# A two-layer encoder trunk on one core: the first FFN input product in two halves of the features, with modulation units 1024 wide

## The reference, cut to what matters

```python
cond = silu(c)
for layer in range(2):
    mod = cond @ w_ada[layer] + b_ada[layer]        # 2048 x 12288, 100 MB a layer
    sh_m, sc_m, g_m, sh_f, sc_f, g_f = split(mod, 6)
    h = rms_norm(x, norm_mix_gain[layer]) * (1 + sc_m) + sh_m
    y = pool_mixer(h) if layer == 0 else hgrn2_mixer(h)   # hgrn: w_in 2048 x 8192, w_out 2048 x 2048
    x = x + g_m * y
    h = rms_norm(x, norm_ffn_gain[layer]) * (1 + sc_f) + sh_f
    a, b = split(h @ w_ffn_in[layer], 2)            # 2048 x 11264
    x = x + g_f * ((silu(a) * b) @ w_ffn_out[layer])      # 5632 x 2048
return rms_norm(x, final_gain)
```

## Time and profile before

| what | us |
| --- | --- |
| median of 3 runs | 2437.61 (2435.35 to 2439.57) |
| the profiled execution | 2439.01, of which the span from first to last instruction is 2437.3 |
| PE busy | 2180.4 (89%), 9905 matmul instructions |
| DVE busy | 1743.5 (72%) |
| ACT busy | 1077.3 (44%) |
| DMA | 573.63 MB, mean 235 GB/s |

### The profile page before, as it was taken

How to read it: one execution, slowest core, us unless ns; L and a number is a source line. 1 busy time by engine, 2 the same in 40 slices (tenths; PEclk the granted TensorE clock), 3 DMA queues, 4 the chain that set the end, 5 groups by cost and what they waited for, 6 DMA issues and landing times. The chain is left out here.

```text
span 2437.3 us, 33187 instructions
## 1 busy us (share of the span) xinstructions
PE 2180.4 (89%) x9905; PEld 1786.8 (73%) x9905; DVE 1743.5 (72%) x2673; ACT 1077.3 (44%) x1803; POOL 9.8 (0%) x43
## 2 busy tenths in 40 slices
PE   1284279999999999989999999898999999999997
PEld 1243268888888787877878787776888888878886
DVE  6868867777776688875969686987555555557675
ACT  2021044444444444445555545544545444444443
POOL 0000000000000000010000000000000000000000
PEclk9997579999999999999999999998999999999999
DMA  8978958888887798975656564685666666667775
GB/s 303 323 247 288 316 161 286 268 276 286 269 275 252 242 325 311 323 248 181 187 168 200 177 188 133 193 298 188 190 191 183 192 185 191 189 214 255 253 257 201
DMA packets 295002, 573.63 MB, mean 235 GB/s; under 512 B 17504, under 2 KB 17632, under 8 KB 294160
## 3 DMA queue, kind: packets, MB, share of 16 engines
q1 hardware_dynamic: 294928, 572.76, 71.9%
HBM read 570.59 MB, written 2.10 MB: 235 GB/s over the span
## 5 line engine op out<-in xcount | busy, mean ns | idle before, releaser
L1041 DVE TENSOR_TENSOR w_lo<-raw,w_hi 128x512 fp32r<-128x512 f32 x1392 | 941.9, 688 | 571.2 <-ACT w_hi L738 566.4
L738 ACT ACTIVATE w_hi<-raw 128x512 fp32r<-128x512 f32 x1392 | 850.8, 629 | 741.9 <-PE prod L484 716.1
L482 PE MATMUL prod<-w_hi,h_hi 128*128 128x512 f32 x2080 | 830.6, 399 | 25.9 <-DVE w_lo L1041 20.4
L484 PE MATMUL prod<-w_hi,h_lo 128*128 128x512 f32 x2080 | 815.2, 392 | 0.0
L483 PE MATMUL prod<-w_lo,h_hi 128*128 128x512 f32 x2080 | 814.6, 392 | 0.0
L482 PEld LDWEIGHTS prod<-w_hi,h_hi 128*128 128x128 f32 x2080 | 393.8, 189 | 123.9 <-DVE w_lo L1041 37.4
L484 PEld LDWEIGHTS prod<-w_hi,h_lo 128*128 128x128 f32 x2080 | 392.9, 189 | 84.1
L483 PEld LDWEIGHTS prod<-w_lo,h_hi 128*128 128x128 f32 x2080 | 393.7, 189 | 79.2 <-issue 1.4
L1075 DVE SCALAR_TENSOR_TENSOR acc<-ada,cond,acc 128x512 f32<-128x512 f32 x536 | 393.5, 745 | 18.3 <-DMA ada<-in_w_ada 16.9
L482 PE MATMUL prod<-w_hi,g_hi 128*128 128x512 f32 x704 | 278.7, 396 | 3.0 <-DVE w_lo L1041 3.0
L484 PE MATMUL prod<-w_hi,g_lo 128*128 128x512 f32 x704 | 274.8, 390 | 0.0
(11 more groups left out here) (124 smaller groups left out, 982.0 us busy)
## 6 DMA issues: line engine op xcount, KB each, us to landing
ada<-in_w_ada SPq DMA_DIRECT2D x384, 512.0 KB, 5.2
raw<-in_w_ffn_in SPq DMA_DIRECT2D x352, 512.0 KB, 4.4
raw<-in_w_ffn_out SPq DMA_DIRECT2D x176, 512.0 KB, 4.9
raw<-in_hgrn_w_in SPq DMA_DIRECT2D x128, 512.0 KB, 3.8
raw<-in_hgrn_w_out SPq DMA_DIRECT2D x32, 512.0 KB, 5.0
raw<-in_pool_w SPq DMA_DIRECT2D x8, 512.0 KB, 7.0
xs<-in_x SPq DMA_DIRECT2D x2, 1024.0 KB, 9.7
out<-xs SPq DMA_DIRECT2D x2, 1024.0 KB, 4.0
```

What stands on the lines that cost most here:

```text
L482: pe.matmul(o, hi(k)[:, ts], wh, start=(k == 0), stop=False)
L484: mm = pe.matmul(o, lo(k)[:, ts], wh, start=False, stop=(k == blocks - 1))
L738: act.activation(split_slot(t, deep)[0], raw[:, r, t.get("step") % 2], ACT.Copy).then_inc(hi_ready, 1)
L1041: dve.tensor_tensor(wl, raw[:, r, t.get("step") % 2], wh, ALU.subtract).then_inc(lo_ready, 1)
```

## The change

The modulation units become 1024 columns wide (24 in all, `UW`): one load is 128 rows x 4 KB, again 512 KB, one fold is 128x1024 into one buffer, and every fold after the first waits for the one before it. The order of the units changes. Eight wide units come ahead of the first FFN (list `HEAD`: shift and scale of the mixer by halves, both gate halves, then only the first half of the FFN's shift and scale). Sixteen are folded behind products at written step numbers (`BEHIND`): 8 in the first FFN, 5 and most of a sixth in HGRN, the rest of that in its output product, 2 in the second FFN.

The first FFN input product runs in two halves of the features. For the first 9 of 11 column groups (`NA`), 18 chunks of 8 steps use features 0 to 1023 and ACT copies each to SBUF (`part_gate`, `part_value`); meanwhile the other half of shift and scale is folded. Then 18 chunks of 8 steps use features 1024 to 2047, and DVE adds the parts (`add_gate`, `add_value`). The last 2 groups run in whole chunks. The work per step on PE is the same.

Weight splits are made on pairs: one ACT and one DVE instruction for 128x1024, a ring of four pairs in every stage. The pooling groups are put between folds, PE multiplies 8 of 16 blocks of the two wide gate units (32 blocks of 512). The transposes of the last hidden group move into the first chunk of the FFN output. All hardware loops are gone; every wait is on a constant.

```diff
-    PE_LOADS = [6] * (NCH - 1) + [KU - ADA]
-    AHEAD = SPL
+    PE_FOLDS = 8
+    AHEAD = 4
+    NA = 9
+    EVAC = 5
...
+    HEAD = [(0, SH_M, 0), (0, SC_M, 0), (0, SH_M, 1), (0, SC_M, 1), (0, G_M, 0), (0, G_M, 1), (0, SH_F, 0), (0, SC_F, 0)]
+
+    BEHIND = [((0, SH_F, 1), A0 + 2, A0 + 50, None), ((0, SC_F, 1), A0 + 56, A0 + 106, A0 + 116),
+              ((0, G_F, 0), A0 + 118, A0 + 172, None), ((1, SH_M, 0), A0 + 180, A0 + 234, None),
+              ((1, SH_M, 1), A0 + 242, A0 + 296, None), ((1, SC_M, 0), A0 + 304, OUT0 + 6, None),
+              ((1, SC_M, 1), OUT0 + 14, OUT0 + 68, None), ((0, G_F, 1), OUT0 + 76, OUT0 + 132, OUT0 + 144),
+              ((1, SH_F, 0), H0 + 20, H0 + 62, None), ((1, SH_F, 1), H0 + 68, H0 + 110, None),
+              ((1, SC_F, 0), H0 + 116, H0 + 158, None), ((1, SC_F, 1), H0 + 164, H0 + 204, None),
+              ((1, G_M, 0), H0 + 210, H0 + 246, None), ((1, G_M, 1), H0 + 254, W0 + 32, W0 + 43),
+              ((1, G_F, 0), OUT1 - 116, OUT1 - 60, None), ((1, G_F, 1), OUT1 + 46, OUT1 + 84, OUT1 + 110)]
...
-            def hi(deep=False):
+            def hi():
...
-                act.activation(split_slot(t, deep)[0], raw[:, r, t.get("step") % 2], ACT.Copy).then_inc(hi_ready, 1)
+                act.activation(w_hi[:, slot], raw[:, r], ACT.Copy).then_inc(hi_ready, 1)
...
+            for c2 in range(2 * NA):
+                def in_a(k):
+                    if c2 == 0:
+                        first_half(k)
+                    second_features()
+                    if c2 and k == EVAC:
+                        take(C_A + c2 - 1, part_of(C_A + c2 - 1), ACT.Copy)
+                chunk(in_a, AHEAD if c2 == 0 else 0)
...
+            def add_gate(j):
+                multiplied(dve, C_B + 2 * j)
+                if j:
+                    dve.wait_ge(small_full[1], t.get("small1"))
+                dve.tensor_tensor(tok[:, :, :], prod[0][:, :, :], part_gate[:, j], ALU.add).then_inc(prod_free[0], 1)
+
+            def add_value(j):
+                multiplied(dve, C_B + 2 * j + 1)
+                pv = part_value[:, j]
+                dve.tensor_tensor(pv, prod[1][:, :, :], pv, ALU.add).then_inc(prod_free[1], 1)
+                dve.wait_ge(silu_ready, j + 1)
+                evacuated(dve, C_B + 2 * j + 1)
+                dve.tensor_tensor(tok[:, :, :], tok[:, :, :], pv, ALU.mult).then_inc(hidden_ready, 1)
```

More of the change, by code:

```diff
@@ L52, in tick @@
         self.n[name] = self.get(name) + k
[L54 to L74, removed]
 def due(step, n, first, last):
@@ L341, in load_chunk @@
-            def load_chunk(src, at, blocks, units=(), shift=0, loaded=0):
-                for s in range(blocks):
-                    if s % 2 == 0 and s >= loaded:
[L345 to L348, removed]
+                    if u:
+                        sp.wait_ge(unit_summed, 2 * u)
+                    for r in range(2):
+                        sp.dma_start(bias[32 * r:32 * r + 1, :],
+                                     b_ada[layer:layer + 1, at + r * CH:at + (r + 1) * CH]).then_inc(bias_loaded, 16)
@@ L507, in reduce_unit @@
[L507 to L520 removed]
+                        after(s)
@@ new lines, in product, with h_product, multiply_loads @@
+                    for u, (_, last) in SPAN.items():
+                        if g == last + SUM:
+                            reduce_unit(u)
+                t.tick("chunk")
+            def h_product(after=None, before=None, first=0):
+                product(h_hi, h_lo, first, after, before)
+            def multiply_loads(u):
+                pe.wait_ge(unit_taken, u)
+                for k in range(PE_FOLDS):
+                    n = u * KD + k
+                    slot = n % ADA
+                    pe.wait_ge(ada_loaded[slot], 16 * (n // ADA + 1))
+                    for o in range(2):
+                        mm = pe.matmul(modp[:, o], cond_rows[:, k], ada[:, slot, o * CH:(o + 1) * CH], start=(k == 0), stop=False)
+                    mm.then_inc(ada_free[slot], 1)
@@ L741, in ahead, with chunk @@
             def ahead():
-                for k in range(AHEAD):
+                for _ in range(AHEAD // 2):
                     hi()
-            def chunk(n, before=None, deep=False, done=0):
-                for k in range(n):
+            def chunk(before=None, done=0):
+                for k in range(STEPS[t.get("chunk")]):
+                    for u, at in TAKE.items():
+                        if t.get("step") == at:
+                            take_unit(u)
                     if before is not None:
@@ new lines, in chunk, with take_unit @@
+                    t.tick("step")
+                t.tick("chunk")
+            def take_unit(u):
+                layer, section, half = UNITS[u]
+                act.wait_ge(unit_reduced, u + 1)
+                if is_gate(u):
+                    earlier = sum(is_gate(v) for v in range(u))
+                    if earlier:
+                        act.wait_ge(x_updated, 2 * earlier)
+                    act.activation(gate[:, :, :], modp[:, :, :], ACT.Copy).then_inc(unit_taken, 1)
+                    return
+                at = (KD if section in (SC_M, SC_F) else 0) + half * UB
+                act.activation(mod[:, 0 if section < SH_F else 1, at:at + UB], modp[:, 0, 0:UB], ACT.Copy).then_inc(unit_taken, 1)
@@ L989, in _ @@
             ahead()
[L990 removed]
+            take(C_WOUT - 1, sg[:, :, :], ACT.Silu)
             t.tick("small0", NL // 2)
@@ L1044, in ahead, with chunk @@
             def ahead():
-                for k in range(AHEAD):
+                for _ in range(AHEAD // 2):
                     lo()
-            def chunk(n, after=None, deep=False, done=0, before=None):
-                for k in range(n):
+            def chunk(after=None, done=0, before=None):
+                for k in range(STEPS[t.get("chunk")]):
                     if before is not None:
                         before(k)
-                    if k >= done:
-                        lo(deep)
+                    if k >= done and k % 2 == 0:
+                        lo()
@@ L1089, in unit @@
-            def unit():
-                for k in range(KD):
-                    fold(k)
-            def norm_prepare(gains, branch):
-                if gains is not None:
-                    dve.wait_ge(unit_taken, t.value("unit"))
-                    dve.scalar_tensor_tensor(gain[:, :], mod[:, branch, KD:2 * KD], 1.0, cols[:, gains:gains + KD],
-                                             ALU.add, ALU.mult)
-                dve.wait_ge(squared, t.value("sq"))
+                    for span in SPAN.values():
+                        for _ in due(t.get("step"), KD, *span):
+                            fold()
@@ L1190, in _, with pool_group @@
             t.tick("sq", NCH * TB)
-            unit()
-            unit()
-            with t.loop(dve, NCH - 1, PER_2UNITS):
-                unit()
-                unit()
-            def pool_group(n, w):
+            def pool_group(n, w, between):
                 src, span, lo_end = padded, 1, 1
-                step = [t.get("pool")]
                 def done(ins):
@@ new lines, in _ @@
+            normalise(3, 1)
+            for _ in range(HG):
+                lo()
+            pool_group(2, WINDOWS[2], nothing)
+            pool_group(3, WINDOWS[3], fold)
+            folds(KD - PE_FOLDS - 7)
+            pool_update(0)
+            pool_update(1)
+            for _ in range(HG):
+                lo()
+            folds(KD - PE_FOLDS)
+            folds(4)
+            pool_update(2)
+            folds(2)
+            pool_update(3)
+            folds(4)
+            norm_root()
```

1155 lines of the change are left out of this document (566 added, 589 removed).

## The result

The kernel after the change takes 2406.86 us (median of 4 runs, 2405.55 to 2407.36), against 2438.59 before in the same runs: a ratio of 0.987, 95% interval 0.9853 to 0.9887. It is faster by 1.3%. 2355 was forecast with a range of 2322 to 2402, so the time lies 5 us above the range and the gain is 32 us of 82. The profiled execution has a span of 2405.6 us.

The account below looks back on a forecast made before the run. The prediction took PE as the bound from 329.6 us on and the modulation units' four-slot load ring in the head. Stages 262 + 500 + 256 + 474 + 114 + 493 + 242 + 14 gave 2355 us, range 2322 to 2402.

Parts of the forecast that it names:

- The head: Start to first FFN product: 262 us, 68 us earlier, by folding 8 wide units, 16 of the old ones, not 20.
- The reading that the ring of four slots sets the pace: Head: load landing plus folds limit the four-slot ring to 1.58 us a load, 25.3 us a wide unit.
- The cross-check by bytes, 263 us: Head: loads of 75.4 MB at the old mean rate of 287 GB/s give 263 us.
- 3 us for stalls: First FFN input: allowance added to 497 us of PE work, giving 500.
- Sum 19.6, 86%: Second halves of first FFN input: DVE work of 19.6 us in 16 steps, 22.8 us of PE.
- the term of 12 us: HGRN: time added because DVE would be 90% busy, in a stage forecast at 474 us against 459.5 before.
- The bounds I gave were 0 and 45: HGRN's added time: 0 if PE hides 90% DVE load as it hides 79%, 45 if the ceiling is 80%.
- The row that I had: Old HGRN output product: two chunks with DVE busy 87% took 53.4 us where PE's own work is 45.3.
- The sign that I had named for being wrong: Second halves or HGRN: PE waiting on `w_lo` for over 20 us in all would show the forecast wrong.
- The rival that code loading would cost 0.7 us a block: Whole span: some 130 blocks of straight code loaded; at 0.7 us each the time is 2446 us; slower, chance 0.04.
- the restarts of the loop go: Second FFN output: with the loop unrolled its restarts vanish, 242 us against 246.5 before.
- DVE binds in HGRN and the second halves: Rival: DVE ceiling at 80 to 85% adds 20 to 45 us in HGRN, 5 to 15 in FFN; 2380 to 2415; chance 0.24.

Follow-up runs that it names:

- e9: Changed kernel with the two halves undone: all ten shift and scale units folded in the head, first FFN input in whole chunks; 2437.2 us, 0.998 of before.
- e4: Changed kernel, second halves of first FFN input reordered: ACT takes hidden blocks at steps 4 and 5, DVE makes their low parts after the gate addition; 2389.2 us.
- e5: e4 with ACT copying the turned q and f blocks in HGRN one step later, after that step's weight split; 2378.1 us, HGRN 494.1.
- e2: Changed kernel with folds of the five units inside HGRN on 64 of 1024 columns, except each unit's first; 2384.8 us, HGRN 480.9.
- e3: e2 with weight splits on single steps in place of pairs; 2368.5 us in a single run, HGRN 471.2.
- e12: Changed kernel with late hidden blocks, later q and f copies in HGRN, single-step splits, and HGRN folds on 64 columns; 2351.1 us, HGRN 464.4.
- e11: e5 with one unit moved from HGRN to the first FFN output and the other four spread wider, pair splits kept; 2365.6 us, 0.9689 of before.

## Why the prediction was wrong, by its steps

**The head (262, measured 266.9): right.** The wide fold was put at 1.28 us and is 1279 ns:

```profile
L1016 DVE SCALAR_TENSOR_TENSOR acc<-ada,cond,acc 128x1024 f32<-128x1024 f32 x292 | 373.5, 1279 | 9.9 <-DMA ada<-in_w_ada 6.8
...
SPq L289 <- DVE feat L1016: 68.5, 50, 3.5
```

The first line is of the whole span, the second of SP's queue in the head; with the folds into the other buffer SP waited 137 us for folds there and 35 for PE at the gate units. The reading that the ring of four slots sets the pace, not DVE and not the DMA engines, fits: DVE is busy for 207 of 267 us, at 299 GB/s. No run has a ring of another depth, so it is not shown. The last fold of the gate units ends at 198 us (195 by the prediction) and the last bias at 260 (255). Run e9 puts the price of two wide units in the head at 50.7 us, 25.4 each; 25.3 was worked out. The cross-check by bytes, 263 us, was luck: it took 75.4 MB at 287 GB/s, and the head moved 79.9 MB at 299, as it also loads the first blocks of the next stage.

**First FFN input (500, measured 517.2): wrong by one term, 3 us for stalls, which were some 20.** All else in that sum was right: with the order of e4 the stage takes 500.8, and the first halves, with ACT's copies of the parts, have PE busy for the whole of the window:

```profile
411.60:491.42 79.82, 79.82 (x369) 66.51 (x368) 56.45 (x56) 41.02 (x45) 0.00 (x0) 1.00 0.82 281
```

The step that failed is "In the second halves DVE has in 16 steps ... Sum 19.6, 86%. I put 3 for stalls". It priced the stalls by DVE's share of busy time. DVE had 18.1 us of work a pair of chunks, less than the 19.6 forecast, and PE stalled all the same. The sum asked how much work DVE has and not what a wait does to the instructions behind it. `take_hidden` stands at steps 1 and 2 of the value chunk, 9 and 10 of the pair; the transposes that it waits for come after step 7 on PE. ACT, up to eight steps ahead, stands still for 7 us and goes on with hardly a lead. Then a pair split needs 1.06 us on ACT and 1.22 on DVE, behind what DVE has queued. The wait alone does not do it. In the second FFN input ACT has a like wait ten times, PE is busy for 492.27 of 492.27 us, and DVE for only 54%:

```profile
ACT g_hi L831 <- PE small L469: 61.2, 10, 6.1
```

**HGRN (474, measured 507.1): wrong in the term of 12 us, which was 45.** The work was right (102.5 us a group, 103.6 measured; the terms as printed add to 101.5). The bounds I gave were 0 and 45, and I took a value near the first "as the ring is four pairs deep". That was the failed choice: the depth of the ring is of no use when ACT has been stopped in front of a transpose, and one pair split ahead of that stop was worth 10.7 us (e5). The row that I had, two chunks with DVE busy for 87% and PE waiting, was the nearer one. The sign that I had named for being wrong, PE waiting for `w_lo` for over 20 us, is there with 44.4. By the runs, of the 47.7 us: fold work 26 (e2), single splits 10 more when there is room (e3), the two early copies 7 more (e12), and 4.9 are left, of which 2.7 were the reductions. The 26 are more than the share of the change, as e2 takes 74 us of DVE work out and the change had put 58 in; in proportion it is 21. Each share holds PE's slower clock with it. In another order the parts weigh otherwise: with all work in place, later copies give 10.7 and one unit less, with the wider spacing, 8.8, both together 25 (e4 to e11). So it is not a sum of a work part and an order part. My reading, which no run isolates further, is that a queue on DVE costs little while ACT has a lead, and a lost lead costs little while DVE is idle.

**The other stages: right.** The output product was forecast at 114 (its printed terms add to 115.3) and took 109.3; of the middle chunks, in which PE waited for low parts before, one runs at PE's pace:

```profile
1601.40:1624.89 23.49, 23.49 (x101) 18.78 (x100) 12.89 (x11) 10.84 (x13) 0.00 (x0) 1.00 0.70 219
```

**Unrolling: right.** The page of the profile counts 77 loads of code on one queue against 33, where the rival had some 130. The second FFN input, now all straight code, has PE busy for 492.27 of 492.27 us. The rival that code loading would cost 0.7 us a block is out. The two FFN stages of the second layer gained 2.5 and 4.4 us. The moved transposes explain the first. The second, forecast by "the restarts of the loop go", has other parts in the trace: before, four narrow gate sums took 3.5 us against 1.75 for the wide one, the granted clock was 0.81 in the first 9.1 us against 1.00 now, and PE waited once, 1.16 us, for a `w_lo`. Whether that wait had to do with the loop is not shown. The Trainium skill ("Runtime: NRT & Kernel Launch", "Instruction fetch mechanics") says that a taken branch stalls when its target lies outside the fetched window. The prediction took from it a stall at each turn of the loop; no run shows where the targets of these loops lay, and the loop of the first FFN had PE busy for 292.00 of 292.00 us.

**The rivals.** The one with 0.24, "DVE binds in HGRN and the second halves", 2380 to 2415, gave the time, and my range took in only its lower two thirds. Its mechanism was half right: in HGRN work and order act together, in the second halves another order alone took the stalls away.

## What to carry to other kernels

An engine that runs ahead in program order can lose its lead at one wait that stands too early. Place a wait for another engine later than the step at which that engine does the work, by up to the lead (here the ring is eight steps deep, and three steps later were enough), and put the next time-critical instruction ahead of it. To tell this from a full engine, look at the engines that feed the late one, and at their waits for each other: in the second halves the same DVE work stalled PE in one order and did not in the other. In the second FFN input, with DVE busy for 54%, waits of ACT nearly as long were free, so the length of a wait does not give its price.

Where the work of a helper engine comes near the main engine's time in a stage with chains across engines (here 90% of it by the forecast), price the stage by the nearest row in which a like share already made the main engine wait, and let the range reach that bound. And look at the main engine's granted clock beside its stalls: of the 26 us by which HGRN fell in e2, 10 were busy time.

## What the runs showed of the hardware

Rows of 4 KB in place of 2 KB cut the packets from 8260 to 4882 for the same 15.9 MB and left the pace of the loads as it was. At 50 to 100 us, before and after:

```profile
DMA packets 8260, 15.93 MB, mean 319 GB/s; under 512 B 488, under 2 KB 488, under 8 KB 8259
```

```profile
DMA packets 4882, 15.89 MB, mean 318 GB/s; under 512 B 489, under 2 KB 489, under 8 KB 4882
...
ada<-in_w_ada SPq DMA_DIRECT2D x27, 512.0 KB, 5.0
```

Landing took 5.0 us against 4.8, with four loads of pooling weights in the same queue. I had put 6.3 us for the ring's cycle, with the landing time of the shorter rows, and e9 has four loads in 6.3 us; no gain of the longer rows is seen.
